# Both feed-forward output projections as seven half-size products in turn, on hidden-block sums made in the input phase

## What is computed

```python
D_MODEL = 1024; SEQ = 1024; D_FF = 2816

def swiglu_ffn(h, w_in, w_out):
    gate, up = jnp.split(h @ w_in, 2, axis=-1)
    return (jax.nn.silu(gate) * up) @ w_out

    f = swiglu_ffn(rms_norm(x, ffn1_pre_g[l]), ffn1_w_in[l], ffn1_w_out[l])
    x = x + 0.5 * rms_norm(f, ffn1_post_g[l])
    ...                                                   # token mixer
    f = swiglu_ffn(rms_norm(x, ffn2_pre_g[l]), ffn2_w_in[l], ffn2_w_out[l])
    x = x + 0.5 * rms_norm(f, ffn2_post_g[l])
```

## Time and profile before

| | us |
|---|---|
| median of 3 runs | 2444.27 |
| lowest, highest | 2443.01, 2446.74 |
| profiled execution | 2442.74 |
| its span on the core | 2440.9 |
| hidden phases, about | 20 to 462, 1750 to 2187 |
| output phases, about | 462 to 710, 2187 to 2431 |

### The profile page before, as it was taken

How to read it: one execution, slowest core, us unless ns; L and a number is a source line. 1 busy time by engine, 2 the same in 40 slices (tenths; PEclk the granted TensorE clock), 3 DMA queues, 4 the chain that set the end, 5 groups by cost and what they waited for, 6 DMA issues and landing times. The chain is left out here.

```text
span 2440.9 us, 31095 instructions
## 1 busy us (share of the span) xinstructions
PE 2384.3 (98%) x11259; PEld 1995.4 (82%) x11259; DVE 1452.9 (60%) x1655; ACT 820.4 (34%) x1191; POOL 1023.0 (42%) x638
## 2 busy tenths in 40 slices
PE   6999999999999999999999999999999999999998
PEld 5888888788888888888888887787788888887886
DVE  6655555446453695686686685642575555544565
ACT  4333333223454224224224232412343333323332
POOL 5545454345552223223223235114464545534464
PEclk9999999999999999999999999999999999999999
DMA  4233222345732123123123135444313222224563
GB/s 146 74 88 92 77 77 77 114 145 186 238 102 66 31 70 91 31 70 91 31 70 92 39 128 200 138 137 146 102 55 96 78 77 77 86 82 161 178 217 121
DMA packets 215989, 254.80 MB, mean 104 GB/s; under 512 B 8821, under 2 KB 161875, under 8 KB 215891
## 3 DMA queue, kind: packets, MB, share of 16 engines
q1 hardware_dynamic: 209363, 240.93, 31.4%
q10 hardware_dynamic: 6528, 12.58, 1.4%
HBM read 197.90 MB, written 55.57 MB: 104 GB/s over the span
## 5 line engine op out<-in xcount | busy, mean ns | idle before, releaser
L585 PE MATMUL PU<-XH,w_h 128*128 128x512 f32 x1008 | 400.1, 397 | 3.3 <-DVE mt L2009 1.3
L587 PE MATMUL PU<-XH,w_l 128*128 128x512 f32 x1008 | 394.0, 391 | 0.0
L586 PE MATMUL PU<-XL,w_h 128*128 128x512 f32 x1008 | 393.6, 390 | 0.0
L2112 POOL TENSOR_TENSOR ws<-pw,ws 128x512 fp32r<-128x512 f32 x176 | 249.3, 1420 | 244.6 <-ACT ws L1178 244.6
L1754 DVE TENSOR_TENSOR hb_l<-hb_raw,hb_h 128x512 fp32r<-128x512 f32 x88 | 206.6, 2349 | 220.6 <-ACT hb_h L1261 220.6
L2157 POOL TENSOR_TENSOR wo_l<-wo_raw,wo_h 128x1024 fp32r<-128x1024 f32 x88 | 215.4, 2449 | 240.8 <-ACT wo_h L1260 240.8
L2107 POOL TENSOR_TENSOR w_l<-w_raw,w_h 128x2048 fp32r<-128x2048 f32 (+1 forms) x40 | 179.0, 4474 | 320.8 <-ACT w_h L1096 320.8
L1851 DVE SCALAR_TENSOR_TENSOR PG<-ub,cw,PG 128x512 f32<-128x512 f32 x464 | 308.0, 750 | 6.1 <-issue 6.1
L2112 POOL TENSOR_TENSOR ws<-s_sum,ws 128x512 fp32r<-128x512 f32 x126 | 165.2, 1313 | 157.9 <-ACT ws L1178 157.9
L585 PEld LDWEIGHTS PU<-XH,w_h 128*128 128x128 f32 x1008 | 190.1, 189 | 46.7 <-issue 6.1
L587 PEld LDWEIGHTS PU<-XH,w_l 128*128 128x128 f32 x1008 | 189.9, 188 | 40.4
(11 more groups left out here) (301 smaller groups left out, 5299.2 us busy)
## 6 DMA issues: line engine op xcount, KB each, us to landing
pw<-in_ffn_w_in SPq DMA_DIRECT2D x88, 512.0 KB, 5.3
wo_raw<-in_ffn_w_out SPq DMA_DIRECT2D x88, 512.0 KB, 3.6
w_raw<-in_w_mix_in SPq DMA_DIRECT2D x50, 512.0 KB, 4.7
hb_raw<-h_d SPq DMA_DIRECT2D x88, 256.0 KB, 4.0
h_d<-hid SPq DMA_DIRECT2D x42, 512.0 KB, 3.1
x_d<-FACC SPq DMA_DIRECT2D x16, 512.0 KB, 3.0
gate_d<-tmp ACTq DMA_DIRECT2D x16, 512.0 KB, 2.8
gt<-gate_d SPq DMA_DIRECT2D x16, 512.0 KB, 5.5
```

The lines of the kernel that those rows point to most:

```text
L585: pe.matmul(dst, hi(k), xh(k), start=(n == 0), stop=False)
L586: pe.matmul(dst, hi(k), xl(k), start=False, stop=False)
L587: last = pe.matmul(dst, lo(k), xh(k), start=False, stop=(n == KT - 1))
L2112: PT(ws[:, i, 1, :, :], form_source(name, par), ws[:, i, 0, :, :], ALU.subtract).then_inc(form_lo, 1)
```

## The change

The output projection too is computed as seven half-size products on halves of tokens, hidden blocks and output columns. A hidden pair m (an even block e and an odd block o, each with token halves 0 and 1) is one step of a product; a product runs over all 11 pairs before the next one begins, in the order P1, P6, P5, P7, P4, P3, P2: 77 steps. The products take three stored blocks (the forms A11, A12, A22) and four sums S1 to S4 of hidden blocks. `hidden_sums` forms the sums on VectorE at the end of each pair of the hidden phase, in `s_buf`, and SP stores them and the blocks to `f_d` (seven forms of 256 KB a pair; the eighth, e0, is not stored).

A step loads one form (256 KB) and, except in P5, one 128x512 quarter of the weights (256 KB). The weights' sums T1, T2 and those of P7 and P4 are made by `step_sum` on VectorE, in P1, P6, P7 and P4, one step ahead of `step_lo`; the weights' quarter B12 is loaded once, in three parts (`b12_load`), and stays on the chip for a phase. Both operands of a step lie side by side, so ScalarE copies 128x1024 and VectorE subtracts 128x1024; GpSimd's part in the steps is gone. There are four raw buffers and four split sets. A product has four PSUM banks, and the other four hold the product before it, which `drain` adds up in `FACC` (P7 into two tiles, so 32 operations a phase). TensorE's loop over steps is written out. P2's last two steps run tile by tile. The post-norms of tiles 0 to 3 are laid between the steps from 57 on, GpSimd's list and the order of loads at the end of the first output phase are rewritten to match.

```diff
-N_P, N_T, N_S, N_H, N_X, N_STEP = 7 * FB - 3, 7 * FB - 7, 4 * FB - 4, 2 * FB, 32, 2 * FB - 4
+N_P, N_T, N_S, N_H, N_X = 7 * FB - 3, 7 * FB - 7, 4 * FB - 4, 2 * FB, 32
+
+NM = FB // 2
+OUT_ORDER = ("P1", "P6", "P5", "P7", "P4", "P3", "P2")
+N_L = len(OUT_ORDER) * NM
+F_A22, F_A12, F_A11, F_S1, F_S2, F_S3, F_S4 = range(1, 8)
+OUT_FORM = {"P1": F_A11, "P6": F_S2, "P5": F_S1, "P7": F_S3, "P4": F_A22, "P3": F_S4, "P2": F_A12}
+OUT_RAW = {"P1": (0, 0), "P6": (1, 1), "P5": None, "P7": (1, 1), "P4": (1, 0), "P3": (1, 1), "P2": (1, 0)}
+SUMMED = ("P1", "P6", "P7", "P4")
+TAILED = ("P2",)
+DRAINED = {"P1": 0, "P6": 4, "P5": 8, "P7": 12, "P4": 20, "P3": 24, "P2": 28}
+N_TSUM, N_OUT, N_DRAIN = len(SUMMED) * NM, 4 * len(OUT_ORDER), 32
+RAWS, SETS = 4, 4
+N_FREED = sum(9 if p in TAILED else 10 for p in OUT_ORDER)
 
...
+            def store_even(n, m, src):
+                sp.wait_ge(hid_ready, N_H * n + 4 * m + 2)
+                sp.dma_start(f_d[ds(m, 1), :, F_A11, :].rearrange("a p t -> p (a t)"), src).then_inc(e_stored, 16)
+
+            def store_odd(n, m):
+                sp.wait_ge(hid_ready, N_H * n + 4 * m + 4)
+                sp.dma_start(f_d[ds(m, 1), :, F_A22:F_A12 + 1, :].rearrange("a p f t -> p (a f t)"),
+                             hid[:, 1, :, :].rearrange("p a t -> p (a t)")).then_inc(o_stored, 16)
+
+            def store_sums(n, m):
+                sp.wait_ge(s_part, 4 * NM * n + 4 * m + 4)
+                sp.dma_start(f_d[ds(m, 1), :, F_S1:F_S4 + 1, :].rearrange("a p f t -> p (a f t)"),
+                             s_buf[:, :, :].rearrange("p f t -> p (f t)")).then_inc(s_stored, 16)
...
+                with sp.Fori(1, NM - 1) as i:
+                    pair_raw(n, 2 * i + 2, 0, wv)
+                    store_even(n, i, hid[:, 0, 1, :])
+                    pair_raw(n, 2 * i + 3, 1, wv)
+                    store_odd(n, i)
+                    store_sums(n, i)
+                store_even(n, NM - 1, hid[:, 0, 1, :])
+                step_load(n, 0, ov)
+                step_load(n, 1, ov)
+                b12_load(n, 0, ov)
+                step_load(n, 2, ov)
+                step_load(n, 3, ov)
+                b12_load(n, 1, ov)
+                b12_load(n, 2, ov)
+                store_odd(n, NM - 1)
+                store_sums(n, NM - 1)
+
+            def weight_rows(ov):
...
+            def step_load(n, l, ov):
+
+                name, m = out_step(l)
+                r, form = l % RAWS, OUT_FORM[name]
+                if l < RAWS:
                     sp.wait_ge(p_done, N_P * n + products_done(FB - 1, "P1"))
                 else:
-                    sp.wait_ge(wo_lo, m - 1)
-                    sp.wait_ge(hb_lo, m - 1)
-                sp.wait_ge(hid_stored[k % 2], blocks_stored(n, k))
-                sp.dma_start(wo_raw[:, m % 2, :], ov[:, k, :]).then_inc(step_full[m % 2], 16)
-                sp.dma_start(hb_raw[:, m % 2, :], h_d[k, :, half * HALF:(half + 1) * HALF])\
-                    .then_inc(step_full[m % 2], 16)
...
+                def block(dst, s, t, first, final):
                     tok = slice(t * P, (t + 1) * P)
-                    col = slice(c * 512, (c + 1) * 512)
-                    pe.matmul(OUTB[t][c], hb_h[r][:, tok], wo_h[r][:, col], start=first, stop=False)
-                    pe.matmul(OUTB[t][c], hb_h[r][:, tok], wo_l[r][:, col], start=False, stop=False)
-                    return pe.matmul(OUTB[t][c], hb_l[r][:, tok], wo_h[r][:, col], start=False, stop=final)
-
-                def operands(m):
-                    pe.wait_ge(wo_lo, 2 * FB * n + m + 1)
-                    pe.wait_ge(hb_lo, 2 * FB * n + m + 1)
-
-                def step(m, slot):
-                    operands(m)
+                    pe.matmul(dst, f_h[s][:, 0, tok], f_h[s][:, 1, :], start=first, stop=False)
+                    pe.matmul(dst, f_h[s][:, 0, tok], f_l[s][:, 1, :], start=False, stop=False)
+                    return pe.matmul(dst, f_l[s][:, 0, tok], f_h[s][:, 1, :], start=False, stop=final)
+
+                def bank_free(q, t):
+
+                    if q == 0:
+                        pe.wait_ge(taken, N_T * (n + 1) - (7, 7, 3, 0)[t])
+                    elif q == 1:
+                        pe.wait_ge(taken, N_T * (n + 1))
+                    else:
+                        before = OUT_ORDER[q - 2]
+                        pe.wait_ge(o_drained, N_DRAIN * n + DRAINED[before] + (2 * t + 2 if before == "P7" else t + 1))
+
+                for l in range(N_L):
+                    name, m = out_step(l)
+                    q, s = l // NM, l % SETS
+                    banks = (XB, YB)[q % 2]
+                    tail = name in TAILED
+                    pe.wait_ge(f_lo, N_L * n + l + 1)
+                    if tail and m == NM - 2:
+                        continue
                     for t in range(4):
...
+                        if m == 0:
+                            bank_free(q, t)
+                        if tail and m == NM - 1:
+                            block(banks[t], (l - 1) % SETS, t, False, False)
+                        last = block(banks[t], s, t, m == 0, m == NM - 1)
...
+            def hidden_sums(n, m, e):
+
+                e0, e1 = e
+                o0, o1 = hid[:, 1, 0, :], hid[:, 1, 1, :]
+                done = 4 * NM * n + 4 * m
+                dve.wait_ge(hid_ready, N_H * n + 4 * m + 4)
+                if n or not isinstance(m, int) or m:
+                    dve.wait_ge(s_stored, 16 * NM * n + 16 * m)
+                TT_(s_buf[:, 0, :], e0, o0, ALU.add).then_inc(s_part, 1)
+                TT_(s_buf[:, 2, :], e1, e0, ALU.subtract).then_inc(s_part, 1)
+                dve.wait_ge(s_part, done + 1)
+                TT_(s_buf[:, 1, :], s_buf[:, 0, :], e1, ALU.subtract).then_inc(s_part, 1)
+                dve.wait_ge(s_part, done + 3)
+                TT_(s_buf[:, 3, :], o1, s_buf[:, 1, :], ALU.subtract).then_inc(s_part, 1)
+
             def hidden_phase(n):
...
+            def step_sum(n, l):
+
+                name, m = out_step(l)
+                if name not in SUMMED:
+                    return
+                b = f_raw[:, l % RAWS, 1, :]
+                dve.wait_ge(f_full[l % RAWS], raw_landed(n, l))
+                if name == "P1":
+                    dve.wait_ge(b12_full[m // 4], 16 * (n + 1))
+                    dve.wait_ge(p_done, N_P * (n + 1))
+                    op = TT_(T1[:, m, :], B12[:, m, :], b, ALU.subtract)
+                elif name == "P6":
+                    dve.wait_ge(t_sum, N_TSUM * n + m + 1)
+                    op = TT_(T2[:, m, :], b, T1[:, m, :], ALU.subtract)
+                elif name == "P7":
+                    op = TT_(b, b, B12[:, m, :], ALU.subtract)
+                else:
+                    dve.wait_ge(t_sum, N_TSUM * n + NM + m + 1)
+                    op = TT_(b, b, T2[:, m, :], ALU.subtract)
+                op.then_inc(t_sum, 1)
+
+            def step_lo(n, l):
+
+                name, m = out_step(l)
+                r, s = l % RAWS, l % SETS
+                dve.wait_ge(f_hi, N_L * n + l + 1)
+                if name in ("P6", "P5"):
+                    TT_(f_l[s][:, 0, :], f_raw[:, r, 0, :], f_h[s][:, 0, :], ALU.subtract)
+                    TT_(f_l[s][:, 1, :], (T2 if name == "P6" else T1)[:, m, :], f_h[s][:, 1, :], ALU.subtract)\
+                        .then_inc(f_lo, 1)
+                else:
+                    TT_(f_l[s][:, :, :], f_raw[:, r, :, :], f_h[s][:, :, :], ALU.subtract).then_inc(f_lo, 1)
+
+            def out_tile(t, c, half):
+                f = (4 * half + t) * D + c * 512
...
+            def drain(n, name, t):
+
+                q, base = OUT_ORDER.index(name), N_DRAIN * n
+                bank = (XB, YB)[q % 2][t]
+                c11, c12, c22, c21 = out_tile(t, 0, 1), out_tile(t, 1, 1), out_tile(t, 1, 0), out_tile(t, 0, 0)
+                dve.wait_ge(o_done, N_OUT * n + 4 * q + t + 1)
+                if name == "P1":
+                    dve.wait_ge(s_stored, 16 * NM * (n + 1))
+                    op = dve.tensor_copy(c11, bank)
+                elif name == "P6":
+                    dve.wait_ge(o_drained, base + t + 1)
+                    op = TT_(c21, bank, c11, ALU.add)
+                elif name == "P5":
+                    dve.wait_ge(o_drained, base + DRAINED["P6"] + t + 1)
+                    op = TT_(c12, bank, c21, ALU.add)
+                elif name == "P7":
+                    dve.wait_ge(o_drained, base + DRAINED["P5"] + t + 1)
+                    TT_(c22, bank, c12, ALU.add).then_inc(o_drained, 1)
+                    op = TT_(c21, bank, c21, ALU.add)
+                elif name == "P4":
+                    dve.wait_ge(o_drained, base + DRAINED["P7"] + 2 * t + 2)
+                    op = TT_(c21, bank, c21, ALU.add)
+                elif name == "P3":
+                    op = TT_(c12, bank, c12, ALU.add)
+                else:
+                    op = TT_(c11, bank, c11, ALU.add)
+                op.then_inc(o_drained, 1)
 
...
```

(80 more changed lines are left out.)

297 lines of the change are left out of this document (124 added, 173 removed).

## The result

| | before | after |
|---|---|---|
| median | 2444.43 us of 4 runs | 2401.73 us of 4 runs |
| lowest, highest | 2443.01, 2446.74 | 2401.47, 2404.3 |
| span of the profiled execution | 2440.9 | 2400.2 |

The ratio is 0.9827, 95% interval 0.9812 to 0.9843: 42.7 us faster by the medians, 40.7 by the spans. The prediction was 2404.0, the range 2390 to 2423. The kernel before, timed again beside the later runs, gave medians of 2443.5 to 2444.0 us, so that a difference of less than about 1 us says nothing.

A forecast was written before the change was run, and what follows sets the result against it. TensorE, busy for 98% of the span, was taken as the bound. Terms of -59.8, -8.8, +17.9, +1.6, +1.1, +4.9 and +3.3 summed to -39.8 us, giving 2404 us from the median; range 2390 to 2423.

The forecast's parts named there:

- 264 fewer matmuls: Output projection, both phases: 924 matmuls a phase in place of 1056, at 0.2267 us each, -59.8 us.
- old starts: Start of each output phase: TensorE's existing waits and half clock all go, -8.8 us.
- new starts: Start of each output phase: new waits for low parts and load 4, plus one loss of clock, +17.9 us.
- stores beside steps: Output phases: stores and residual loads beside eight steps need 385 GB/s, +0.8 us a phase, +1.6 in all.
- first pair: Hidden phase's first pair: four added VectorE operations make U2 late for P7, +1.1 us once.
- end of the first: First output phase's end: post-norms bunch up, so scale(7) comes late for TensorE's transposes, +4.9 us (bounds 0 and 8).
- end of the second: Kernel's end: last post-norm 10.4 us behind the last matmul, where it was 7.1, +3.3 us.
- The other engines: Output-phase steps: VectorE needs 1.8 of 2.72 us, low part 1.2, ScalarE's copy 1.06; TensorE stays the bound.
- (c): Rival, summed products: loads set the pace through the three-step loop; slower, 2460 us at a 7.5 us landing; chance 0.05.
- (d): Rival, whole change: another matmul count than 924 a phase, or added work binds from the start; 2444 us; chance 0.03.
- (a): Rival, phase starts and ends: they cost little, load 4 lands in time, scale(7) is ready; 2389 us; chance 0.11.
- (b): Rival, hidden loop: U2 late, 1 us beyond its slack in each of 18 pairs; 2422 us; chance 0.12.

The follow-up runs named there:

- e7: Two more 128x512 VectorE operations a pair in the hidden phase, on data nobody reads, added to the changed kernel: 2421.18 us.
- e4: Three raw buffers in place of four in the changed kernel: 2428.35 us.
- e6: One more 128x1024 GpSimd subtraction, unread, beside each of steps 2 to 56 of both output phases of the changed kernel: 2540.4 us.
- e12: Tile 5's gain multiplied on VectorE instead of GpSimd, in the changed kernel: 2398.67 us.
- e9: Both ends reordered (ScalarE squares, GpSimd roots, tile 7's drain earlier), on the changed kernel with VectorE's start order changed and loads 4 to 7 earlier: 2390.9 us.
- e10: The mixer pre-norm's four scalings (tiles 4 to 7) moved from ScalarE to VectorE behind the last post-norm, on e9: 2387.84 us.

## Why the prediction was right

The total came out within 2.3 us of the median. By its terms, each from the trace of after:

| term | predicted | found |
|---|---|---|
| 264 fewer matmuls | -59.8 | -59.8 |
| old starts | -8.8 | -8.8 |
| new starts | +17.9 | +10.8 |
| stores beside steps | +1.6 | +0.5 |
| first pair | +1.1 | +1.5 |
| end of the first | +4.9 | +9.7 |
| end of the second | +3.3 | +4.9 |
| sum | -39.8 | -41.2 |

The spans differ by 40.7. The terms from the old starts to the first end are recorded idle times and half clock, and miss some 0.3 us for each short wait (e7). By the distances of TensorE's starts beyond 0.2267 us the old starts are -9.7, the new ones +11.7, the wait at step 66 +0.8, the first pairs +2.1, the end of the first +9.3 and that of the second +4.8; with the -59.8 this closes at -40.8. **The matmuls** were right in count and price; in mid-product their starts lie 0.2267 us apart, so the rows, and not the 215.7 ns of the Trainium skill's page, gave the term. **The other engines** kept up as worked out, 1.25 us for the low part and no wait in mid-product; rivals (c) and (d) have nothing for them. e4 shows that the loop of (c) exists, but with one buffer less it costs about 4 us of the 27 lost; what binds there is the queue's order at the starts and VectorE's drains. Rival (a) did not occur either: load 4 did not land in time, and `scale(7)` was late. e6 shows that the choice of 1.2 over 2.4 us was the one on which the gain hung: dropping GpSimd's part made room for VectorE's.

**The stores beside steps** had the wrong mechanism. The term was for transfers that can't pass in time; the one wait there (step 66) comes from VectorE, busy with a post-norm operation that GpSimd had lengthened from 1.28 to 5.65 us.

**The starts** were over-priced by 7.1 us. The first wait came as stated (3.8 predicted, 3.50 in the record; the starts lie 3.89 us apart in place of 0.23, so 3.7). Load 4 landed at 474.8 (predicted 474). But I had added the half clock and the later waits, and they lie on top of one another: with step 2 at half speed TensorE comes to step 3 late, when its low part is almost there, and waits 0.29 us, not 2.2. In return the clock fell at both starts, not at one: waits of 3.8 + 4.0 at steps 2 and 3, clock 1.6 + 1.4.

**The first pair.** U2 starts at 92.00, P7 at 92.73, where it was 92.09: 0.64 late. I had counted one such place. The second phase has the same, and a small wait for ScalarE's copy stands before each (0.51 and 0.59).

**The first end** was under-priced by half. The chain was the predicted one, up to `scale(7)` as releaser, but sizes were off. `post(7)` ends 18.2 us behind the last matmul (predicted 15): VectorE's two operations on tile 4 take 6.6 us and not 2.5, since GpSimd's multiplication and its low part run beside them (e12). From there to the end of `scale(7)` it took 6.6 us (predicted 6); ScalarE's other scalings stand in this stretch, but only where the post-norms end earlier does its list set the time (e9, e10). The wait is 8.3 us; before, it was 0.3. The half clock behind such a wait was in no term: the 16 transposes take 3.57 us, where 16 at full clock took 1.91 before. **The second end** closes with the last post-norm 11.8 us behind the last matmul (predicted 10.4): VectorE waits 2.26 us for GpSimd's product with the drain of tile 7 queued behind it. e12 takes this wait away; e9 takes only the drain out from behind it, and a wait of 1.66 us is left.

So two errors in opposite directions, 7.1 us at the starts and 6.4 at the two ends, cancelled. That the total hit to 2.3 us is luck in this part. The hit is that of a sum whose large term was sure; the small ones, the stores apart, were right in place and only about half right in size. Rival (b) did not occur, but by a margin of 0.8 us. e7 shows its price to be higher than I gave: 0.4 us beyond the margin cost 0.56 a pair, and 1.2 us of work turned into 19 us in all.

## What to carry to other kernels

When work leaves the bound engine, read the margins it leaves elsewhere and treat each one as a number to be kept: here the margin was 0.8 us in a loop of 18 pairs, and 1.2 us of added work cost 10 us in the loop and 19 in all. Waits in a row (an engine's order, then a queue that follows it) must be taken away together, since removing the first alone can make it worse; and a wait that follows at once behind half clock is partly covered by it, so the two are not added. An engine that is off the critical path is not free, if its operation holds up another's.
